# Differential attention on one core: the output norm's scales spread by two products of rounded parts instead of one fp32 product

## The reference, cut to what matters

```python
def rmsnorm(x, g):
    xf = x.astype(jnp.float32)
    y = xf * lax.rsqrt(jnp.mean(xf * xf, axis=-1, keepdims=True) + EPS)
    return (y * g.astype(jnp.float32)).astype(x.dtype)
...
        s = jnp.einsum('ibhqd,ibhkd->ibhqk', qblk, kh) + bias
        p = jax.nn.softmax(s, axis=-1)
        a = p[0] - lam * p[1]
        return jnp.einsum('bhqk,bhkv->bhqv', a, vh)
...
    o = rmsnorm(o, g_norm) * (1.0 - lambda_init)
```

## Time and profile before

| | us |
|---|---|
| median of 3 runs | 3427.72 |
| lowest, highest | 3424.59, 3429.3 |
| span of the profiled execution | 3421.6 |
| median of the runs less that span | 6.1 |
| PE busy | 3279.7 (96%) |
| DVE busy | 2014.6 (59%) |
| ACT busy | 1324.5 (39%) |
| POOL busy | 1223.2 (36%) |

### The profile page before, as it was taken

The page is one execution under the profiler, slowest core; times in us unless marked ns, Lnnn a source line. Parts: engine busy times, 40 slices in busy tenths (PEclk is TensorE's granted clock), DMA queues, the critical chain, the costliest instruction groups (busy, mean ns, idle before and its releaser), DMA issues. The chain is left out here.

```text
span 3421.6 us, 51012 instructions
## 1 busy us (share of the span) xinstructions
PE 3279.7 (96%) x19032; PEld 2553.4 (75%) x19032; DVE 2014.6 (59%) x4689; ACT 1324.5 (39%) x2165; POOL 1223.2 (36%) x511
## 2 busy tenths in 40 slices
PE   7999999999999999999999988999999988999998
PEld 6888888877777777787777764666666556888887
DVE  3322312227556655665567788888888556556654
ACT  3111111114333433343333335666666555233332
POOL 3322313244333333333333326777777533000000
PEclk9999999999999999999999999999999999999999
DMA  6545445555454544544448964121221266666562
GB/s 213 182 156 184 167 153 167 179 200 182 137 176 136 184 146 129 183 145 137 130 160 288 324 215 139 59 75 55 73 65 38 99 218 234 222 234 231 181 216 77
DMA packets 317907, 554.90 MB, mean 162 GB/s; under 512 B 35421, under 2 KB 114525, under 8 KB 317662
## 3 DMA queue, kind: packets, MB, share of 16 engines
q1 hardware_dynamic: 266510, 471.26, 42.8%
q10 hardware_dynamic: 51152, 80.38, 6.5%
HBM read 382.03 MB, written 169.50 MB: 161 GB/s over the span
## 5 line engine op out<-in xcount | busy, mean ns | idle before, releaser
L731 POOL TENSOR_TENSOR glaf_w_lo<-early_raw,glaf_w_hi 128x1024 fp32r<-128x1024 f32 x140 | 350.7, 2506 | 650.3 <-ACT glaf_w_hi L705 650.3
L760 PE MATMUL glaf_dense_acc<-h_hi,glaf_w_hi 128*128 128x512 f32 x1120 | 452.7, 404 | 4.1 <-ACT glaf_dense_out L714 4.1
L760 PE MATMUL glaf_dense_acc<-h_lo,glaf_w_hi 128*128 128x512 f32 x1120 | 439.0, 392 | 0.0
L760 PE MATMUL glaf_dense_acc<-h_hi,glaf_w_lo 128*128 128x512 f32 x1120 | 436.8, 391 | 0.0
L1749 DVE CUSTOM_DVE_ANT_0 front_p<-diff_s_ps,ahead_table 128x512 f32<-128x512 f32 x544 | 346.7, 686 | 54.2 <-PE diff_s_ps L1611 53.0
L514 POOL TENSOR_TENSOR proj_w_lo<-early_raw,proj_w_hi 128x1024 fp32r<-128x1024 f32 x84 | 204.4, 2436 | 477.7 <-DVE proj_w_hi L476 477.7
L1572 POOL TENSOR_SCALAR front_p<-front_p,diff_ratio 128x1024 f32<-128x1024 f32 (+1 forms) x80 | 270.1, 3377 | 174.9 <-DVE diff_ratio L1769 174.9
L1692 ACT ACTIVATE front_p<-front_p,diff_neg_max 128x2048 f32<-128x2048 f32 (+1 forms) x160 | 278.9, 1744 | 10.1 <-DVE diff_neg_max L1759 10.0
L1635 PE MATMUL diff_oT_ps<-diff_aT,diff_v 128*128 128x512 f32 x544 | 273.8, 604 | 6.0 <-ACT diff_aT L1686 6.0
L201 PE MATMUL proj_acc<-h_hi,proj_w_hi 128*128 128x512 f32 x672 | 262.8, 391 | 0.0
L1610 PE MATMUL diff_s_ps<-ahead_k,ahead_q_high 128*128 128x512 f32 x544 | 245.1, 451 | 18.3 <-DVE diff_mx L1749 10.7
(11 more groups left out here) (216 smaller groups left out, 7167.6 us busy)
## 6 DMA issues: line engine op xcount, KB each, us to landing
early_raw<-in_w_zg SPq DMA_DIRECT2D x180, 512.0 KB, 4.8
early_raw<-in_w_stream SPq DMA_DIRECT2D x80, 512.0 KB, 3.7
scratch_zg<-glaf_dense_out SPq DMA_DIRECT2D x140, 256.0 KB, 2.3
items_raw<-in_w_br SPq DMA_DIRECT2D x120, 256.0 KB, 2.9
merge_gate<-scratch_zg SPq DMA_DIRECT2D x120, 256.0 KB, 3.1
scratch_featT<-proj_out ACTq DMA_DIRECT2D x80, 256.0 KB, 2.3
items_br_hi<-scratch_item_hi SPq DMA_DIRECT2D x60, 256.0 KB, 5.9
items_br_lo<-scratch_item_lo SPq DMA_DIRECT2D x60, 256.0 KB, 6.4
```

The source lines that it names most:

```text
L731: pool.tensor_tensor(self.w_lo[:, s], self.raw[:, u % self.RAW], self.w_hi[:, s], ALU.subtract).then_inc(self.lo_split, 1)
L760: done = pe.matmul(self.acc[:, u % self.banks], a, x, start=i == 0, stop=i == self.PER - 1)
```

## The change

The 128x4 scales are split on DVE into a rounded part (`scale_hi`, a cast to fp32r) and the rest (`scale_lo`), two more steps of the chain. POOL builds two diagonals instead of one, written as fp32r. PE multiplies a matrix of ones in fp32r (`ones_r`, set once) with both, one product after the other into the same accumulator, where there was one fp32 product. The waits count the two diagonals.

```diff
-        diag = m.sb("diag", [P, G, P])
+        diag_hi, diag_lo = (m.sb(f"diag_{s}", [P, G, P], FP32R) for s in ("hi", "lo"))
...
+        ones_r = m.sb("ones_r", [P, P], FP32R)
+        scale_hi, scale_lo = m.sb("scale_hi", [P, G], FP32R), m.sb("scale_lo", [P, G])
...
-        NORM_STEPS = 2 + RSQRT_STEPS
+        NORM_STEPS = 4 + RSQRT_STEPS
...
             pool.memset(ones[:, :], 1.0).then_inc(ones_ready, 1)
+            pool.memset(ones_r[:, :].bitcast(FP32), 1.0).then_inc(ones_ready, 1)
...
                     pool.wait_ge(norm_steps, (g + 1) * NORM_STEPS)
                     pool.wait_ge(spread, g)
-                    pool.tensor_tensor(diag[:, :, :], ident[:, :].unsqueeze(1).broadcast_to([P, G, P]),
-                                       stat[:, 2].unsqueeze(2).broadcast_to([P, G, P]), ALU.mult).then_inc(diag_ready, 1)
+                    for diag, part in ((diag_hi, scale_hi[:, :].bitcast(FP32)), (diag_lo, scale_lo[:, :])):
+                        pool.tensor_tensor(diag[:, :, :], ident[:, :].unsqueeze(1).broadcast_to([P, G, P]),
+                                           part.unsqueeze(2).broadcast_to([P, G, P]), ALU.mult).then_inc(diag_ready, 1)
...
                 if g == 0:
-                    pe.wait_ge(ones_ready, 1)
+                    pe.wait_ge(ones_ready, 2)
...
             def spread_scale(g):
-                pe.wait_ge(diag_ready, g + 1)
-                pe.matmul(n_ps[:, :], ones[:, :], diag[:, :, :].rearrange("p g c -> p (g c)"), start=True, stop=True).then_inc(spread, 1)
+                pe.wait_ge(diag_ready, 2 * g + 2)
+                pe.matmul(n_ps[:, :], ones_r[:, :], diag_hi[:, :, :].rearrange("p g c -> p (g c)"), start=True, stop=False)
+                pe.matmul(n_ps[:, :], ones_r[:, :], diag_lo[:, :, :].rearrange("p g c -> p (g c)"), start=False, stop=True).then_inc(spread, 1)
...
                 if g:
-                    dve.wait_ge(diag_ready, g)
+                    dve.wait_ge(diag_ready, 2 * g)
...
                 rsqrt_by_psum(step, dve, stat[:, 2], var, tmp)
+                step(dve.tensor_copy(scale_hi[:, :], stat[:, 2]))
+                step(dve.tensor_tensor(scale_lo[:, :], stat[:, 2], scale_hi[:, :].bitcast(FP32), ALU.subtract))
```

## The result

| | before | after |
|---|---|---|
| median of 15 runs (us) | 3428.23 | 3434.39 |
| lowest, highest | 3423.76, 3431.27 | 3429.04, 3437.77 |
| span of the profiled execution | 3421.6 | 3427.2 |

A forecast was written before the change was run, and what follows sets the result against it. DVE bounds groups 0 to 2, PE groups 3 to 17 with DVE close behind, then a drain. +0.5 + 2.8 + 1.0 + 0.6 = +4.9 us gave a median of 3432.6, range 3427.5 to 3437.5.

The forecast's parts named there:

- PE's gain is offered and lost at the pinch: Middle groups: PE's spread saves 0.38 us each, 5.7 for 15, but DVE's new steps turn it into +0.5.
- the pinch: Middle groups, after the spread: a DVE bias pass releases PE's score product, with 0.18 us to spare.
- the prediction's room: Middle groups: PE may come early by at most 0.34 + 0.18 = 0.52 us less DVE's new steps.
- the wait ahead of the pinch: Middle groups: DVE's third bias pass after the norm waits for PE, 0.34 us to spare.
- (c): Middle groups: PE's saving comes through, -5.7 us instead of +0.5, in all -1.3, 3426.4; chance 0.09.
- (e): The fp32r pair isn't shorter than the fp32 product: 1.3 us more in the drain, 3434; chance 0.07.
- The cast is held by POOL: Middle groups: the cast waits until POOL's sum ends, so DVE's two steps take 0.55 us instead of 0.40.
- rival (b): Middle groups: POOL doesn't hold the cast, 0.40 us per norm, -2.3 against the sum, 3430.3; chance 0.18.
- Groups 0 to 2: DVE-bound first stretch: 1.2 us each in groups 0 and 1, 0.40 in group 2, together +2.8 (2.2 to 3.4).
- the first bound: Groups 0 and 1: the scaling slips between the diagonals, only the combination waits for the low one; +0.9 us.
- rival d: Middle groups: the two diagonals reach DVE's scaling; at 1.6 us per diagonal +6.6, in all +11.5, 3439; chance 0.10.
- Drain: Groups 18 and 19, finished with little beside them: +1.0 us for group 18 and +0.6 for group 19.

The follow-up runs named there:

- one rounded product: Kernel before, with one fp32r diagonal and one fp32r product, the scales' low part left out: 3425.78 us, ratio 0.9992.
- cast from PSUM: Changed kernel, with the norm's last step writing the scales into PSUM, where the cast and subtraction read them: 3432.21 us, ratio 1.0015.
- early gate: Changed kernel, with the gate product of groups 0 to 17 moved from DVE to POOL, ahead of POOL's far half: 3426.23 us, ratio 0.9997.
- the early gate alone: Kernel before, with the gate product of groups 0 to 17 moved from DVE to POOL, ahead of POOL's far half: 3431.46 us, ratio 1.0011.
- the middle groups only: Groups 3 to 17 as changed, their gate product on POOL ahead of its far half; other groups as before: 3422.43 us, ratio 0.9982.
- behind the far half: Kernel before, with the gate product of groups 0 to 17 on POOL after its far half: 3582.76 us, ratio 1.0458.

## Why the prediction was right, and where it wasn't

The sum was +4.9 us of phase; the two profiles of the changed kernel give +7.6 and +7.5 against the kernel before, the medians +6.2, within the range given. Of the 7.6, 3.0 are a term that the sum lacks; the other pieces give +4.7. That the time lies in the range even so is luck in part: the range had been widened for the scatter of the runs, not for such a term.

- **PE's gain is offered and lost at the pinch.** Right. The pair holds PE for 0.47; one spread to the next is 37.76 instead of 37.72 (+0.04, forecast +0.03; as the mean from norm 4 to norm 17, +0.02). Four runs measure the room: without new steps on DVE 0.15 of 0.62 came through (one rounded product), with steps of 0.40 it was 0.12 a group (cast from PSUM), with steps of 0.54 nothing, and with DVE relieved all of the 0.39 (early gate). So the prediction's room, 0.52 less the steps, holds only for steps of over 0.34, which use up the wait ahead of the pinch; with none it is the 0.18 at the pinch itself. Rivals (c) and (e) fall.
- **The cast is held by POOL.** Right: 0.31 to the end of POOL's sum, the two steps 0.54 (forecast 0.55). The PSUM source shows that without the hold the middle would have been as in rival (b).
- **Groups 0 to 2.** The sum was right (+2.87 for +2.8), its parts less so: alone, the steps cost 1.50 (forecast 1.2) and the second diagonal 1.34 (forecast 1.6). In group 0 the first bound held: the scaling had its turn between the diagonals, 0.40 for the steps and 0.37 for the combination, 0.77 together where that bound had 0.9 and 1.2 were taken. The rest must come from further on, where other collisions differ: at 2084.13 a scaling took 1.21 which took 0.18 at the same place before, while its neighbours were held less. I didn't take these apart.
- **The diagonals don't reach the scaling in the middle** (rival d). Right: one with fp32r written takes 1.04, as one in fp32 does.
- **Drain.** Right: +1.56 for +1.6, though the terms of group 19 (0.40, 1.04, less 0.9) add up to 0.54 and not to the 0.6 written.
- **The step that failed is a term that isn't there**: +2.96 between norms 3 and 4. The prediction read the stretch from 2143 us at a granted clock of 1.00 and had no term for a change of the clock. The opening of group 3 stands behind a wait of 2 us, and there the clock fell to 0.50. The fall goes with the shift of work in groups 0 to 2, in seven profiles against four; what exactly decides is open, and so is how many of the executions without a profile had it. PE's wait before it is 1.96 to 2.00 us in all eleven, so it isn't that wait's length alone. Nor is it that group 3 comes later: norm 3 is 0.5 us sooner than before with the early gate alone, which has the fall, and 0.7 later with the middle groups only, which hasn't.

## What to carry to other kernels

A shorter instruction on an engine that is 99% busy can be worth next to nothing by itself: look for the next engine's place with the least to spare in the same cycle (here DVE had 0.18 us to spare at the pinch and 0.34 in the wait ahead of it, and got 0.54 of new steps), and relieve that in the same edit. Apply such an edit where its engine is the bound and leave the stretches alone where another is: here 15 of 20 groups, with DVE's gate product moved, made +6.2 us into -6.6. A helper operation that is moved to an idle engine should stand ahead of that engine's long work, or the consumers wait for that too (here 3582.76 us behind the far half, 3431.46 ahead of it).

## What the runs showed of the hardware that I had not expected

- PE's clock after the same wait of 2 us: 1.00 throughout in four profiles, down to 0.50 for 3 to 7 us in seven, at a cost of 1.5 to 3.2 us of the phase.
- A VectorE instruction that waits for GpSimd had its turn between two GpSimd instructions of the same queue that had nothing to wait for between them: the scaling in group 0 took 0.92 with one diagonal and with two.
- Moving the cast's source from SBUF to PSUM took all of its waiting away (1.60 us at the most before, 0.16 after).
